# Mixture-of-experts stage: head reordered, down projection as three products of high and low parts, half of the output emptied by VectorE

## The chip, the cores and the metric

One Trainium2 (trn2) chip, one core. The time is that of one whole execution of the program on the device, in microseconds (us). Of the kernel before there are three timed runs, and one more execution that was profiled. All engines have in-order queues and meet at semaphores. TensorE (PE) multiplies, VectorE (DVE), ScalarE (ACT) and GpSimd (POOL) work elementwise, SyncE (SP) issues most of the DMAs.

## The reference

The model is a stack of blocks over 512 tokens of width 1024: a gated-delta mixer, a mixture of experts, sparse attention, a second mixture of experts, and two further layers. The change touches the mixture of experts alone, which runs twice. Its reference, cut down:

```python
def hier_moe(x, w_grp, b_grp, w_rt, b_rt, w_gate, w_up, w_down):
    xt = x.reshape(b * t, d)                        # 512 x 1024
    grp_p = softmax(xt @ w_grp + b_grp)             # 4 groups, the best one is taken
    grp_prob, grp_idx = lax.top_k(grp_p, 1)
    e_logits = ...                                  # 4 experts of that group
    top_p, top_i = lax.top_k(softmax(e_logits), 2)  # 2 of them per token
    gate = ...                                      # weight of each of 16 experts
    for wg, wu, wd, ge in experts:                  # 16 of them, hidden width 256
        hdn = silu(xt @ wg) * (xt @ wu)
        y += ge[:, None] * (hdn @ wd)
    return y
```

All of it is float32. The kernel computes an expert only for the tokens that chose it.

## The kernel before, in words

`stage_experts` runs a whole mixture-of-experts layer. The pairs (token, expert), 1,024 of them, are laid into **blocks** of 128 slots. Every expert has a block of its own, and more are added only for an expert with more than 128 tokens; in the profiled execution there are 16 blocks in each of the two layers (32 fetches of rows, 32 activations). So about half of the 2,048 slots hold no token.

**Head.** SP first issues the constants, the input weights of block 0 (two units of 1 MB), the store of h to `h_rows` in HBM (2 MB), the down weights of block 0 (1 MB) and the vectors `rt.loads` of the layer norm behind the stage. It then waits for `x_loaded[0]`, the rows of block 0, before it issues the weights of block 1 (L1873 to L1876). `Route.slots`, `rows`, `tables` and `tokens` on VectorE work out which token sits in which slot: PE multiplies one-hot rows (`in_row`, which lies in `rt.y`) with `named` (L1648) and so finds the token of every slot, and `tokens` turns that into row numbers `tok`. A slot without a token gets the number of some real row. After `tokens` VectorE makes the low parts of both weight units of block 0. GpSimd's `fetch` (L2023) copies one column of `tok` into `mine`, runs one further small operation, and issues an indirect DMA that brings 128 rows of 4 KB.

**Loop.** Five in-order queues run over the blocks (`pairs`: two unrolled, a loop of pairs, two at the end); buffers alternate by parity. A float32 product is made of three products in the format fp32r: x and w are each split in a high part (a copy by ScalarE that rounds to fp32r) and a low part (the rest, a subtraction), and PE adds xh wh + xh wl + xl wh. In the turn of block i the engines do, in this order:

- PE: 24 matmuls for gate and up of block i (L1951, `gu`), 8 transposes of the rows of block i+1 (L1930), the **down projection of block i-1** (L1942: 4 matmuls in plain float32, which the profile shows as 8 records), 2 transposes of the hidden layer of block i (L1964).
- ScalarE: the hidden layer of i-1 out of PSUM into `ht` (L1984), the high parts of the two weight units of block i+1 (L1789), silu (L2006), the high parts of the rows of i+1 (L1989), and the output of i-1 out of PSUM in two halves (`take`, L1996).
- VectorE: the low part of weight unit 0 of i+1 (L1793), the product of the hidden layer (L2071), the low parts of the rows of i+1 (L2062). Behind block 1 it also works out the gate weights and scales h (L2082).
- GpSimd: the fetch of rows two blocks ahead, and the low part of weight unit 1 of i+1 (L1793).
- SP: the output halves of block i to `moe_rows` (L1881), the down weights of i+2 (`store_and_load_down`, L1887), then the two input units of i+5 into the buffers that the low parts of i+3 have freed (`turn_over`, L1892).

The calls of SP's queue stand in this order in the loop:

```python
store(i)
sp.wait_ge(y_done, i(2, 2))
ws.load_down(sp, b, expert(i.plus(2)))
...
sp.wait_ge(ws.lo_ready[1], i(1, -1))
ws.load_in(sp, b, 1, e)
```

## Time and profile before

| what | value |
|---|---|
| three timed runs | 2580.58, 2588.68, 2588.92 us; median 2588.68 |
| the profiled execution | 2579.54 us, its span 2577.7 us, mean granted TensorE clock 0.948 |
| busy in the span | PE 90%, weight loads 70%, VectorE 45%, ScalarE 41%, GpSimd 33% |
| first expert layer | about 545 to 751 us of the span |
| second expert layer | about 1166 to 1371 us |
| HBM | 293.62 MB read, 31.60 MB written |

The two layers together are 16% of the span. The granted clock is given as a share of full speed (1.0 is 2.4 GHz, 0.5 is 1.2 GHz). A row of the timeline reads: start in us from the span's start, duration, engine, line, operation, output <- inputs, shape, count, and in brackets how long the engine had been idle and what ended that. "SPq" is the DMA queue of SyncE; its rows are issues, not transfers. Matmul records are modelled, so that the distance between starts tells the pace, not the duration of one.

### The profile page before, as it was taken

The page shows a single profiled execution, that of the slowest core. Times are in us where ns is not written, and L with a number is a line of the kernel's source. Part 1 is how long each engine was busy: PE and PEld are TensorE (multiplying, and loading weights), DVE is VectorE, ACT ScalarE, POOL GpSimd, SP SyncE. Part 2 cuts the span into 40 slices and gives each one's busy share as a digit, 9 for nine tenths or more (in the row PEclk, how much of TensorE's full clock was granted, in tenths as well). Part 3 has the DMA queues.
Part 4 walks back from the last instruction along what each step waited for, and adds up shares of the span by engine and source line. Part 5 has one row for each costly group of instructions (what it writes and reads, how often), then busy time and mean ns, then how long its engine had stood idle before and what let it go on. Part 6 is the DMA issues. An engine that isn't in the chain of part 4 may idle for free. (4 is left out here: it accounts for less than half of the span.)

```text
span 2577.7 us, 32698 instructions
## 1 busy us (share of the span) xinstructions
PE 2332.3 (90%) x12304; PEld 1810.2 (70%) x12304; DVE 1147.9 (45%) x2271; ACT 1047.9 (41%) x1830; POOL 853.7 (33%) x375
## 2 busy tenths in 40 slices
PE   6999999759969989995994899999997999999998
PEld 5888888656747866674763667678886767668886
DVE  3654642354436358754434453562223354462122
ACT  4443442216643247723664334533223334533222
POOL 2433532415552310023562222334332312224442
PEclk9999999769989999996997999999999999999999
DMA  6113110239983331017995311224222511315212
GB/s 138 49 50 115 42 50 30 90 137 393 401 296 84 135 105 44 30 51 261 396 406 191 102 49 62 90 67 147 97 66 76 172 33 50 119 50 164 98 66 74
DMA packets 190956, 327.15 MB, mean 127 GB/s; under 512 B 52544, under 2 KB 103056, under 8 KB 178528
## 3 DMA queue, kind: packets, MB, share of 16 engines
q1 hardware_dynamic: 183904, 300.08, 34.2%
q0 software_dynamic: 6912, 25.17, 2.6%
q8 instruction: 92, 1.51, 0.2%
q14 instruction: 48, 0.39, 0.0%
HBM read 293.62 MB, written 31.60 MB: 126 GB/s over the span
## 5 line engine op out<-in xcount | busy, mean ns | idle before, releaser
L159 POOL TENSOR_TENSOR branch_weights_wl<-branch_weights_wf,branch_weights_wh 128x2048 fp32r<-128x2048 f32 (+1 forms) x66 | 301.8, 4574 | 770.7 <-ACT branch_weights_wh L153 770.7
L153 ACT ACTIVATE branch_weights_wh<-branch_weights_wf 128x2048 fp32r<-128x2048 f32 (+1 forms) x66 | 124.6, 1889 | 200.2 <-PE merge_acc L207 92.9
L544 POOL TENSOR_TENSOR in_weights_wl<-in_weights_wf,in_weights_wh 128x1024 fp32r<-128x1024 f32 x32 | 79.5, 2486 | 237.1 <-ACT in_weights_wh L540 219.3
L207 PE MATMUL bmid_acc<-xh,branch_weights_wh 128*128 128x512 f32 x320 | 148.7, 465 | 9.1 <-PEq L72 9.1
L207 PE MATMUL merge_acc<-xh,branch_weights_wh 128*128 128x512 f32 x384 | 152.3, 397 | 3.4 <-PEq L72 3.4
L159 POOL TENSOR_TENSOR nsa_weights_wl<-nsa_weights_wf,nsa_weights_wh 128x2048 fp32r<-128x2048 f32 x13 | 59.5, 4585 | 282.2 <-ACT nsa_weights_wh L153 282.2
L207 PE MATMUL merge_acc<-xl,branch_weights_wh 128*128 128x512 f32 x384 | 152.1, 396 | 0.0
L207 PE MATMUL merge_acc<-xh,branch_weights_wl 128*128 128x512 f32 x384 | 152.0, 396 | 0.0
L207 PE MATMUL bmid_acc<-xh,branch_weights_wl 128*128 128x512 f32 x320 | 127.4, 398 | 0.0
L207 PE MATMUL bmid_acc<-xl,branch_weights_wh 128*128 128x512 f32 x320 | 127.3, 398 | 0.0
L1942 PE MATMUL exp_ps_y<-rt_wf,exp_ht 128*128 128x512 f32 x256 | 115.4, 594 | 2.9 <-ACT exp_ht L1984 1.9
L3274 ACT ACTIVATE bmid_pt<-bmid_x 128x256 f32<-128x256 f32 (+3 forms) x128 | 55.8, 436 | 141.6 <-PE bmid_x L3241 141.6
L568 PE MATMUL gmain_acc<-xh,in_weights_wh 128*128 128x512 f32 x256 | 110.6, 432 | 0.0
L1793 POOL TENSOR_TENSOR rt_wl<-rt_wf,rt_wh 128x2048 fp32r<-128x2048 f32 x16 | 76.9, 4804 | 79.8 <-ACT rt_wh L1789 79.8
L568 PE MATMUL gmain_acc<-xl,in_weights_wh 128*128 128x512 f32 x256 | 102.0, 398 | 0.0
L568 PE MATMUL gmain_acc<-xh,in_weights_wl 128*128 128x512 f32 x256 | 101.8, 398 | 0.0
L3611 ACT ACTIVATE merge_gate<-merge_acc,merge_gb 128x512 f32<-128x512 f32 x48 | 33.1, 689 | 148.8 <-DVE merge_merged L3639 75.2
L3637 DVE TENSOR_TENSOR merge_gate<-merge_gate,merge_b 128x512 f32<-128x512 f32 x32 | 22.0, 687 | 159.9 <-PE merge_b L3563 159.7
L207 PEld LDWEIGHTS merge_acc<-xh,branch_weights_wh 128*128 128x128 f32 x384 | 72.3, 188 | 21.3 <-issue 4.2
L1951 PE MATMUL exp_ps_gu<-rt_wh,xl 128*128 128x512 f32 x256 | 86.6, 410 | 0.4 <-DVE xl L2062 0.4
L207 PEld LDWEIGHTS merge_acc<-xh,branch_weights_wl 128*128 128x128 f32 x384 | 72.3, 188 | 17.3
L207 PEld LDWEIGHTS merge_acc<-xl,branch_weights_wh 128*128 128x128 f32 x384 | 72.4, 189 | 17.2
(659 smaller groups left out, 6209.0 us busy)
## 6 DMA issues: line engine op xcount, KB each, us to landing
branch_weights_wf<-w_in SPq DMA_DIRECT2D x56, 1024.0 KB, 5.1
rt_wf<-moe_w_out SPq DMA_DIRECT2D x32, 1024.0 KB, 10.2
rt_wf<-moe_w_in SPq DMA_DIRECT2D x32, 1024.0 KB, 9.2
in_weights_wf<-gdn_w_in SPq DMA_DIRECT2D x64, 256.0 KB, 3.4
nsa_weights_wf<-moe_w_in SPq DMA_DIRECT2D x16, 1024.0 KB, 9.9
moe_rows<-rt_y SPq DMA_DIRECT2D x64, 256.0 KB, 8.9
branch_weights_wf<-moe_w_in SPq DMA_DIRECT2D x16, 1024.0 KB, 9.8
merge_bwf<-w_branch SPq DMA_DIRECT2D x12, 1024.0 KB, 5.0
```

The lines of the kernel that those rows point to most:

```text
L153: act.activation(self.h[u][:, :, 0:self.cols(b)], self.s.f[u][:, :, 0:self.cols(b)], ACT.Copy).then_inc(self.s.hi_ready, 1)
L159: pool.tensor_tensor(self.l[u][:, :, 0:self.cols(b)], self.s.f[u][:, :, 0:self.cols(b)], self.h[u][:, :, 0:self.cols(b)].bitcast(F32), ALU ...
L207: mm = pe.matmul(self.acc[:, s, 0:cols], lhs[:, P * s:P * s + P], rhs, start=(u == 0 and k == 0 and n == 0), stop=(u == 1 and k == HALF - ...
L544: pool.tensor_tensor(self.l[n % 3][:], self.f[n % 3][:], self.h[n % 3][:].bitcast(F32), ALU.subtract).then_inc(self.lo_ready, 1)
L568: mm = pe.matmul(self.acc[:, tile % 3, :], w[n % 3][:, k, P * s:P * s + P], x[:, HALF * u + k, :], start=(u == 0 and k == 0 and m == 0), s ...
L1793: eng.tensor_tensor(self.l[b][u][:], self.f[b][u][:], self.h[b][u][:].bitcast(F32), ALU.subtract).then_inc(self.lo_ready[u], 1)
L1942: mm = pe.matmul(ps_y[:, c, :], ht[:, k, :], w[:, k, c, :], start=(k == 0), stop=(k == 1))
L1951: mm = pe.matmul(ps_gu[:, 0, :].rearrange("p (c n) -> p c n", c=2), x[:, HALF * u + k, :], ws.by_matrix(w[b][u])[:, :, k, :], start=(u == ...
L3274: act.activation(self.pt[:, e, 0:width], self.ps_t[:, 0:width], ACT.Copy).then_inc(self.copied, 1)
L3611: act.activation(gate[:, f % 2, :], ws.acc[:, f, :], ACT.Sigmoid, bias=gb[:, n, 4 * j + f:4 * j + f + 1]).then_inc(ws.evicted, 1)
L3637: dve.tensor_tensor(gate[:, f % 2, :], gate[:, f % 2, :], ps_b[:, f, :], ALU.mult).then_inc(b_out, 1)
```

## The change

1. **Route.** `in_row` and `named` are now fp32r tensors of their own, so that the eight matmuls that find the tokens run in fp32r. `tokens` gives a slot without a token the number 2T - 1, which no row has, and `fetch` passes `bounds_check=T - 1, oob_is_err=False`: such a slot is skipped. `xr` is set to zero once for this.
2. **Head.** SP issues the input weights of block 1 before the wait for `x_loaded[0]`, and both down loads and the norm vectors behind it. The first two fetches use `tok` itself as their offsets (`fetch_first`). VectorE makes the low part of weight unit 0 of block 0 before `tokens`, then `tokens`, then `tables`, then the low part of unit 1.
3. **Down projection.** `ht` becomes `hth` and `htl`, the down weights become `dh` (copied by ScalarE, `down_hi`) and `dl` (subtracted by VectorE, `down_lo`), both in the room of `g.xh`, one buffer for both parities. PE runs 12 fp32r matmuls where there were 4 in float32. `down_hi` of block i waits until the down projection of i-1 is done.
4. **Output.** ScalarE empties half 0, VectorE half 1.
5. **Waits.** The down load of i+2 waits for `dl_out` of block i instead of `y_done`, still behind `store(i)`. GpSimd's wait for `picked` counts two less, for the two fetches without it.

```diff
-        self.marks, self.in_row = marks, rt.y[:].rearrange("p (n r) -> p n r", r=P)
+        self.marks, self.in_row = marks, st.sb("in_row", [P, 2 * TT, P], F32R)
...
-        link(dve.tensor_scalar(self.spare[:], tok, 0.0, self.marks[:, P + n:P + n + 1], ALU.is_equal, ALU.mult))
+        link(dve.tensor_scalar(self.spare[:], tok, 0.0, 2.0 * T, ALU.is_equal, ALU.mult))
...
-                ws.load_down(sp, 0, 0)
+                for u in range(2):
+                    ws.load_in(sp, 1, u, 1)
+                sp.wait_ge(x_loaded[0], 16)
+                for b in range(2):
+                    ws.load_down(sp, b, b)
                 for x, src in rt.loads:
                     sp.dma_start(x, src).then_inc(ln_in, 16)
-                sp.wait_ge(x_loaded[0], 16)
-                for u in range(2):
-                    ws.load_in(sp, 1, u, 1)
-                ws.load_down(sp, 1, 1)
...
                 def store_and_load_down(i, b):
                     store(i)
-                    sp.wait_ge(y_done, i(2, 2))
+                    sp.wait_ge(dl_out, i(1, 1))
                     ws.load_down(sp, b, expert(i.plus(2)))
...
-                            mm = pe.matmul(ps_y[:, c, :], ht[:, k, :], w[:, k, c, :], start=(k == 0), stop=(k == 1))
+                            for m, (x, w) in enumerate(((hth, 0), (hth, 1), (htl, 0))):
+                                mm = pe.matmul(ps_y[:, c, :], x[:, k, :], by_k[w][:, k, c, :],
+                                               start=(k == 0 and m == 0), stop=(k == 1 and m == 2))
...
+                def down_hi(b, loads, i):
+                    act.wait_ge(ws.loaded[b][2], loads(16))
+                    if not i.is_first():
+                        act.wait_ge(y_done, i(2))
+                    act.activation(dh, ws.f[b][2][:], ACT.Copy).then_inc(dh_out, 1)
...
+                def fetch_first(b):
+                    pool.indirect_dma_start(xr[b][:], None, g.h_rows[:, :],
+                                            bass.IndirectOffsetOnAxis(route.tok[:, b:b + 1], 0),
+                                            bounds_check=T - 1, oob_is_err=False).then_inc(x_loaded[b], 16)
...
+                def hidden_lo(i):
+                    dve.wait_ge(hth_out, i(1, 1))
+                    dve.tensor_tensor(htl[:].rearrange("p k n -> p (k n)"), ps_t[:, 0, 0:HID],
+                                      hth[:].rearrange("p k n -> p (k n)").bitcast(F32), ALU.subtract).then_inc(htl_out, 1)
+
+                def down_lo(b, i):
+                    dve.wait_ge(dh_out, i(1, 1))
+                    dve.tensor_tensor(dl, ws.f[b][2][:], dh.bitcast(F32), ALU.subtract).then_inc(dl_out, 1)
+
+                def take(i):
+                    dve.wait_ge(y_done, i(2, 2))
+                    if not i.is_first():
+                        dve.wait_ge(y_stored[1], i(16))
+                    dve.tensor_copy(y[:, 512:D], ps_y[:, 1, :]).then_inc(y_out[1], 1)
...
                 def body(j, b, i, last):
+                    if not i.is_first():
+                        hidden_lo(i.plus(-1))
                     if not last:
                         ws.lo(dve, 1 - b, 0, i.plus(2))
...
+                    if not i.is_first():
+                        take(i.plus(-1))
+                    down_lo(b, i)
```

**Where instructions moved.** SyncE at the head of the first expert layer; `wf` and `rt_wf_0`, `rt_wf_1` are the input weights of blocks 0 and 1, `rt_wf_2` the down weights. Before:

```order
L1781 DMA nsa_weights_wf<-moe_w_in 128x2048
L1868 DMA h_rows<-h 128x4x1024
L1781 DMA nsa_weights_wf<-moe_w_in 128x2048
L1785 DMA rt_wf_2<-moe_w_out 128x2048
L1872 DMA nsa_weights_ln_vectors<-ln_ffn_g 128x1024
L1872 DMA nsa_weights_ln_vectors<-ln_ffn_b 128x1024
L1872 DMA nsa_weights_norm_gain<-by_feature 128x8
L1872 DMA nsa_weights_norm_shift<-by_feature 128x8
L1781 DMA rt_wf_0<-moe_w_in 128x2048
L1781 DMA rt_wf_1<-moe_w_in 128x2048
L1785 DMA rt_wf_2<-moe_w_out 128x2048
```

And of the change:

```order
L1781 DMA nsa_weights_wf<-moe_w_in 128x2048
L1870 DMA h_rows<-h 128x4x1024
L1781 DMA nsa_weights_wf<-moe_w_in 128x2048
L1781 DMA rt_wf_0<-moe_w_in 128x2048
L1781 DMA rt_wf_1<-moe_w_in 128x2048
L1785 DMA rt_wf_2<-moe_w_out 128x2048 x2
L1878 DMA nsa_weights_ln_vectors<-ln_ffn_g 128x1024
L1878 DMA nsa_weights_ln_vectors<-ln_ffn_b 128x1024
L1878 DMA nsa_weights_norm_gain<-by_feature 128x8
L1878 DMA nsa_weights_norm_shift<-by_feature 128x8
```

The wait for the first rows stands ahead of the row `x2` now; it stood ahead of `rt_wf_0`. Four issues of norm vectors moved behind it.

ScalarE in the turns of blocks 0 and 1, from the rows' high parts to the output (`xl` is the room of the rows' parts, L2006 and L2015 are silu). Before:

```order
L1989 ACTIVATE xl<-exp_ps_x 128x512 x2
L1984 ACTIVATE exp_ht<-exp_ps_t 128x256
L1789 ACTIVATE nsa_weights_wh<-nsa_weights_wf 128x2048 x2
L2006 ACTIVATE exp_act_g<-exp_ps_gu 128x256
L1989 ACTIVATE xl<-exp_ps_x 128x512 x2
L1996 ACTIVATE rt_y<-exp_ps_y 128x512 x2
```

And of the change:

```order
L1999 ACTIVATE xl<-exp_ps_x 128x512 x2
L1994 ACTIVATE xh<-rt_wf_2 128x2048
L1988 ACTIVATE exp_hth<-exp_ps_t 128x256
L1789 ACTIVATE nsa_weights_wh<-nsa_weights_wf 128x2048 x2
L2015 ACTIVATE exp_act_g<-exp_ps_gu 128x256
L1999 ACTIVATE xl<-exp_ps_x 128x512 x2
L2005 ACTIVATE rt_y<-exp_ps_y 128x512
L1994 ACTIVATE xh<-rt_wf_2 128x2048
```

The copy of the down weights, L1994, stands at the end of every turn, ahead of the hidden layer and of the high parts for the next block.

VectorE at the same place, from the low part for block 2 on. Before:

```order
L1793 TENSOR_TENSOR nsa_weights_wl<-nsa_weights_wf,nsa_weights_wh 128x2048
L2071 TENSOR_TENSOR exp_hid<-exp_act_g,exp_ps_gu 128x256
L2062 TENSOR_TENSOR xl<-exp_ps_x,xl 128x512 x2
L1755 TENSOR_REDUCE exp_sg<-exp_eg 128x4
L1756 SCALAR_TENSOR_TENSOR exp_sg<-exp_e,exp_sg 128x4
L1757 RECIPROCAL nsa_weights_weight<-exp_sg 128x4
L1758 TENSOR_TENSOR nsa_weights_weight<-nsa_weights_weight,exp_e 128x4
L2082 TENSOR_SCALAR h<-h 128x1024 x4
```

And of the change:

```order
L2088 TENSOR_TENSOR exp_htl<-exp_ps_t,exp_hth 128x256
L1793 TENSOR_TENSOR nsa_weights_wl<-nsa_weights_wf,nsa_weights_wh 128x2048
L2109 TENSOR_TENSOR exp_hid<-exp_act_g,exp_ps_gu 128x256
L2083 TENSOR_TENSOR xl<-exp_ps_x,xl 128x512 x2
L2099 COPY rt_y<-exp_ps_y 128x512
L2093 TENSOR_TENSOR xh<-rt_wf_2,xh 128x2048
L1755 TENSOR_REDUCE exp_sg<-exp_eg 128x4
L1756 SCALAR_TENSOR_TENSOR exp_sg<-exp_e,exp_sg 128x4
L1757 RECIPROCAL nsa_weights_weight<-exp_sg 128x4
L1758 TENSOR_TENSOR nsa_weights_weight<-nsa_weights_weight,exp_e 128x4
L2121 TENSOR_SCALAR h<-h 128x1024 x4
```

VectorE has three operations more in each turn, and the scaling of h now stands ahead of the low part of a hidden layer (L2088 of the next turn), on which PE's down projection waits.

## Rows read from the trace of the kernel before

**Rows 1.** The stretches view, 640 to 660: busy us per engine, clock, DMA share, GB/s.

```profile
640.00:660.00 20.00, 20.00 (x85) 13.99 (x84) 8.01 (x8) 13.10 (x16) 12.12 (x9) 1.00 1.02 416
```

**Rows 2.** The instructions in order of time: TensorE in one block's turn (start, us, engine, line).

```profile
641.57 0.48 PE L1951 MATMUL exp_ps_gu<-nsa_weights_wh,xl 128*128 128x512 f32 x1
...
647.16 1.03 PE L1930 MATMUL exp_ps_x<-ident,exp_xr 128*128 128x128 f32 x8
...
648.03 3.60 PE L1942 MATMUL exp_ps_y<-rt_wf,exp_ht 128*128 128x512 f32 x8
...
651.60 0.48 PE L1951 MATMUL exp_ps_gu<-rt_wh,xl 128*128 128x512 f32 x1
```

**Rows 3.** The same view, 548 to 590 us: the head of the first expert layer.

```profile
548.58 1.83 SPq L1872 DMA_DIRECT2D nsa_weights_ln_vectors<-ln_ffn_g  x1
...
564.60 0.18 DVE L1736 CAST exp_tok<-exp_spare 128x24 int32<-128x24 f32 x1
...
564.93 2.09 POOL L2024 TENSOR_TENSOR exp_mine<-exp_tok,exp_zero 128x1 int32<-128x1 int32 x1 [61.19 <-DVE exp_tok L1736]
...
569.40 1.12 POOL L2027 DMA_INDIRECT exp_xr<-h_rows,exp_mine  x1 [0.17 <-issue]
...
573.87 0.80 SPq L1781 DMA_DIRECT2D rt_wf<-moe_w_in  x2
...
576.52 0.77 PE L1951 MATMUL exp_ps_gu<-nsa_weights_wh,xl 128*128 128x512 f32 x1 [0.65 <-DVE xl L2062]
...
584.79 1.03 PE L1930 MATMUL exp_ps_x<-ident,exp_xr 128*128 128x128 f32 x8
584.91 1.91 ACT L1789 ACTIVATE rt_wh<-rt_wf 128x2048 fp32r<-128x2048 f32 x1 [1.67 <-DMA rt_wf<-moe_w_in]
...
586.98 4.53 POOL L1793 TENSOR_TENSOR rt_wl<-rt_wf,rt_wh 128x2048 fp32r<-128x2048 f32 x1 [9.47 <-ACT rt_wh L1789]
588.14 0.38 ACT L2006 ACTIVATE exp_act_g<-exp_ps_gu 128x256 f32<-128x256 f32 x1
...
589.88 0.76 PE L1951 MATMUL exp_ps_gu<-rt_wh,xl 128*128 128x512 f32 x1 [0.22 <-DVE xl L2062]
```

**Rows 4.** The same view, TensorE, second expert layer: the end of its first block.

```profile
1203.94 1.03 PE L1930 MATMUL exp_ps_x<-ident,exp_xr 128*128 128x128 f32 x8
```

**Rows 5.** The same view, ScalarE, second expert layer: the first activation.

```profile
1208.54 0.38 ACT L2006 ACTIVATE exp_act_g<-exp_ps_gu 128x256 f32<-128x256 f32 x1
```

**Rows 6.** The same view, 599 to 603 us, VectorE: scaling of h behind block 1.

```profile
600.03 2.50 DVE L2082 TENSOR_SCALAR h<-h 128x1024 f32<-128x1024 f32 x4
```

**Rows 7.** The same view, 636 to 651 us: the other engines in one block's turn.

```profile
636.05 4.84 POOL L1793 TENSOR_TENSOR nsa_weights_wl<-nsa_weights_wf,nsa_weights_wh 128x2048 fp32r<-128x2048 f32 x1 [3.66 <-ACT nsa_weights_wh L1789]
...
641.04 0.33 SPq L1781 DMA_DIRECT2D nsa_weights_wf<-moe_w_in  x1
...
642.12 0.38 ACT L1984 ACTIVATE exp_ht<-exp_ps_t 128x256 f32<-128x256 f32 x1
...
642.39 3.72 ACT L1789 ACTIVATE rt_wh<-rt_wf 128x2048 fp32r<-128x2048 f32 x2
...
643.65 0.36 SPq L1785 DMA_DIRECT2D rt_wf<-moe_w_out  x1
...
644.34 2.29 DVE L1793 TENSOR_TENSOR rt_wl<-rt_wf,rt_wh 128x2048 fp32r<-128x2048 f32 x1 [4.66 <-ACT rt_wh L1789]
...
646.19 4.86 POOL L1793 TENSOR_TENSOR rt_wl<-rt_wf,rt_wh 128x2048 fp32r<-128x2048 f32 x1 [3.77 <-ACT rt_wh L1789]
```

**Rows 8.** DMA issues of the page: bytes each and median us from issue to landing.

```profile
branch_weights_wf<-w_in SPq DMA_DIRECT2D x56, 1024.0 KB, 5.1
rt_wf<-moe_w_out SPq DMA_DIRECT2D x32, 1024.0 KB, 10.2
```

**Rows 9.** The instructions in order of time: the last two down projections of the first expert layer.

```profile
739.22 3.67 PE L1942 MATMUL exp_ps_y<-rt_wf,exp_ht 128*128 128x512 f32 x8 [1.05 <-issue]
...
743.95 3.67 PE L1942 MATMUL exp_ps_y<-rt_wf,exp_ht 128*128 128x512 f32 x8 [0.84 <-ACT exp_ht L1984]
```

60 lines of the change are left out of this document (34 added, 26 removed).

## Prediction, made before the change was run

> **What bounds the kernel now.** I read the page first, for the place of the two expert layers in the span; then the stretches view inside one of them; then the instructions in order of time through one turn of the loop, through the head and through the tail. Blocks are counted from 0.
>
> In the loop two things are full at once. TensorE is busy in 20.00 of 20 us at granted clock 1.00, that is 2.4 GHz, and the DMA share is 1.02 at 416 GB/s [rows 1]. A turn of TensorE is 10.03 us, from one first matmul to the next: 5.59 us for the 24 fp32r matmuls, 0.87 for the transposes, 3.57 for the down projection with the two transposes behind it [rows 2]. From the down projection of block 5 (648.03) to that of block 14 (739.22) are 9 turns: 10.13 us each [rows 2, 9]. TensorE waits for nothing there, so it sets the turn. The DMAs do not lag enough to be waited for, but a down load takes 10.2 us to land [rows 8], where a load of the same size in a calmer stage takes 5.1 [rows 8].
>
> In the head TensorE waits for a chain: `tok` at 564.78; a copy of one column on GpSimd that lasts 2.09 us, beside VectorE's low part; the fetch, issued at 569.40; SP, which waited for the rows, issues at 573.87; first matmul at 576.52. Block 1 waits for its weights, issued only at 573.87: the second high part begins at 584.91, silu at 588.14, gate and up of block 1 at 589.88, though those of block 0 had ended at 584.79 [rows 3].
>
> **The change, part by part.**
>
> *Rows of block 0.* Route in fp32r shortens the token matmuls, but VectorE puts a low part of 2.29 us [rows 7] between them and `tokens`, and saves waiting instead: `tok` comes some 0.8 us earlier at most. The two small GpSimd operations go: the fetch is issued with `tok`, near 564.1 instead of 569.40. The queue is empty then (the same 6 MB lie ahead as before). I take 5.3 us.
>
> *Weights of block 1.* They are issued some 25 us earlier and land before the rows do, so their high parts hide beside block 0. Gate and up of block 0 end at 584.79 - 5.3 = 579.5, silu is over 0.6 later at 580.1; before at 588.52 [rows 3]. Gain 8.4 us. Second layer: 1203.94 - 5.3 + 0.6 = 1199.2 against 1208.92 [rows 4, 5], gain 9.7. I take the table load ahead of silu as hidden; if not, 1.3 less each. **Head: -18.1 us.** SP pays: down loads and norm vectors are issued behind the wait; one norm issue takes 1.83 us [rows 3]. The weights of block 2 therefore go out at the time they do now, and are not late.
>
> *Behind block 1.* VectorE now does `down_lo` (2.29) and the scaling (2.50 [rows 6], and about 0.8 of small operations before it) ahead of the low part of the hidden layer (about 0.4), all behind ScalarE's `down_hi` (1.91 for this shape [rows 3]): 7.9 us from the end of the last down projection. TensorE is ready for the next after 6.5 (5.59 + 0.87 and a transpose [rows 2]). A stall of 1.4 us in each layer: **+2.8**. It has no cover any more; before, nobody waited for the scaling.
>
> *The matmuls themselves.* 12 fp32r matmuls at 5.59/24 = 0.233 us are 2.80, in place of about 3.43: 0.63 off a turn, so TensorE alone would turn in 9.4 us. Less is fetched too: half of the slots, some 0.26 MB of 4.2 a turn.
>
> *The ring that the loop becomes.* This is the term that decides. The down load of i+2 still stands behind `store(i)`, but is wanted earlier: `down_hi` of i+2 comes right after the down projection of i+1, a turn later, where TensorE wanted it nearly two turns later. Behind `down_hi` on ScalarE stand the hidden layer and both high parts for block i+4; behind those GpSimd's low part; behind that on SP the input load, the next stores, the next down load but one. One way round is two turns:
> - from the end of GpSimd's low part (636.05 + 4.84 = 640.89) to the issue of the down load (643.65): 2.76 [rows 7];
> - its landing L;
> - `down_hi` 1.91, `down_lo` 2.29, low part of the hidden layer 0.4, VectorE's low weights 2.29: 6.9. ScalarE's second high part is ready already at 1.91 + 0.27 + 3.72 = 5.9 [rows 7];
> - GpSimd's low part: 4.53 alone [rows 3].
>
> If GpSimd can start only when VectorE's is over, the ring is 14.1 + L. The rows say so: begun 0.44 us before VectorE's ends, it takes 4.86, 0.33 more than alone [rows 3, 7], and the copy of one column took 2.09 [rows 3]. L: ahead of and with the down load lie an input load, two stores, a fetch and itself, 2.9 MB, at 416 GB/s [rows 1] 6.9 us from the input load's issue at 641.04, 2.6 us before the down load's [rows 7]; 4.3 remain, and a fixed part of at most 5.1 - 2.5 = 2.6 [rows 8]; I take 2.0. L = 6.3, nearest to the calm 5.1. The turn is (14.1 + 6.3)/2 = 10.2, against 10.13: over 14 turns and two layers **+2**. The 0.63 that TensorE saves is lost in the ring.
>
> The Trainium skill, in SBUF - State Buffer, section "Who interferes with whom", speaks against this change: a VectorE instruction with two SBUF inputs and a GpSimd instruction that reads SBUF exclude each other for the whole instruction, and the change adds one of 2.29 us a turn. By the rule the ring is the 14.1 + L above; without it (GpSimd starting at 5.9 and taking 4.53) 13.1 + L, a turn of 9.7 and a time some 14 us shorter. The trace agrees with the rule, with the 2.09 us.
>
> *Tail.* The last down projection follows the one before by 1.06 us (743.95 after 739.22 + 3.67) [rows 9]. Now `down_hi`, `down_lo` and the hidden low part stand between: 4.6 and about 0.2 of handing over, +3.7; both projections are shorter by some 0.8, but one of these lies in the turn already counted: +3.7 - 1.6 = **+2.1** a layer, **+4.2**.
>
> The second `take` moves to VectorE, which has room; it gives ScalarE back a part of `down_hi`. I cost it at nothing: TensorE's own work hides it. VectorE was busy 8.01 of 20 us [rows 1].
>
> **Sum:** -18.1 + 2.8 + 2 + 4.2 = about -9. The profiled execution took 2579.54, so 2570.5; the median of the runs shown is 9.1 above that execution. Against the median: 2588.7 - 9 = **2580**. A measurement here can tell about 0.3%, 8 us, from no change, so the sum lies on that edge.
>
> **Bounds of the unknown.** L from 5.1 to 10.2 [rows 8]. At 5.1 the turn is 9.6. At 10.2 it would be 12.1, but that landing belongs to a queue that is always full; a slower ring empties it. I hold L = 8.3, half-way up, for the far end: 11.2.
>
> **Rivals.**
> - *The ring opens.* L about 5.1, TensorE nearly sets the turn at 9.6: 28 turns save 15 us where I add 2. -26, **2563**. For it: less is fetched, and the queue has gaps. Against: the load is issued right behind an input load and two stores.
> - *Late down loads: slower than before.* L = 8.3 makes the turn 11.2, 28 x 1.07 = +30 instead of +2: +19, **2608**. ScalarE would stand at `down_hi` for the DMA in every second turn, and everything behind it. The whole is slower from a turn of 10.13 + 11/28 = 10.5, that is L = 6.9. For it: the 10.2 of now; against: the demand falls from 4.2 to 3.9 MB a turn.
> - *Slots aren't skipped.* If the fetch moves all 128 rows whatever the bound, L grows by 0.6 and the turn by 0.3: +9, **2588**, no change. The packets of the fetch tell it.
>
> **Chances.** The forecast 0.42, on the edge: half faster by over 0.3%, half within, a little slower. The ring opens 0.22. Late loads 0.22. Not skipped 0.08, within. The rest 0.06, a clock that falls in the new pauses of TensorE among it (it is granted 1.00 now [rows 1]), slower. So faster 0.43, same 0.28, slower 0.29. The forecast's own range, with L from 5.8 to 6.9, is 2573 to 2588. The range for 8 in 10 reaches into both rivals: 2562 to 2606.
>
> **What would show it.** Right: first matmul of an expert layer 5 us earlier, silu of block 0 8 to 10 earlier; a down projection of 12 records in about 2.8 us; ScalarE's copy of the down weights idle before it, released by the DMA, for 1 to 2 us in many turns; TensorE waiting before the down projection for the low part of the hidden layer or of the weights; turns near 10.2, perhaps alternating; DMA share below 1.0; GpSimd's low part near 5 us; about 4.8 us before the last down projection. Wrong: `down_hi` never waits for a DMA, or a turn far from 10.2, or a head gain under 6 us a layer.

## The result, and the profile after

| | us | 95% interval of the ratio |
|---|---|---|
| before, median of 4 runs beside the change | 2588.48 (2580.58 to 2588.92) | |
| after, median of 4 runs | 2630.39 (2624.99 to 2633.58) | 1.0167 (1.0141 to 1.0193) |
| after, the profiled execution | 2630.14, span 2628.3, mean clock .942 | |

The change makes the kernel slower by 42 us, 1.7%. The forecast was 2580, the range 2562 to 2606: both were wrong, and the sign with them.

To find the place I cut each expert layer at four kinds of record: the issue of the load of `marks` (the stage begins), the first silu, the fourth and the sixteenth, and the copy into `exp_mx`, which waits for the last store (the stage ends). In the first layer of the kernel before, two of them are these, in the view of the instructions in order of time (start us, duration us, engine, line, operation, tiles; in brackets the idle time before and what ended it); the silu are those of the same form as in [rows 3, 5]:

```profile
545.30 0.35 SPq L1866 DMA_DIRECT2D exp_marks<-c_marks  x1
...
750.55 0.15 DVE L2086 COPY exp_mx<-exp_tm 128x1 f32<-128x1 f32 x1 [11.51 <-DMA moe_rows<-rt_y]
```

And after the change:

```profile
548.40 0.35 SPq L1868 DMA_DIRECT2D exp_marks<-c_marks  x1
...
581.34 0.39 ACT L2015 ACTIVATE exp_act_g<-exp_ps_gu 128x256 f32<-128x256 f32 x1 [2.88 <-PE exp_ps_gu L1955]
...
599.85 0.39 ACT L2015 ACTIVATE exp_act_g<-exp_ps_gu 128x256 f32<-128x256 f32 x1 [0.47 <-PE exp_ps_gu L1955]
...
618.32 0.39 ACT L2015 ACTIVATE exp_act_g<-exp_ps_gu 128x256 f32<-128x256 f32 x1
...
754.03 0.38 ACT L2015 ACTIVATE exp_act_g<-exp_ps_gu 128x256 f32<-128x256 f32 x1
...
776.06 0.15 DVE L2127 COPY exp_mx<-exp_tm 128x1 f32<-128x1 f32 x1 [2.26 <-DMA moe_rows<-rt_y]
```

Differences of such starts give the account, here for both layers (first / second, us):

| | head: to silu of block 0 | block 0 to 3 | block 3 to 15 | tail | stage |
|---|---|---|---|---|---|
| before | 42.8 / 42.1 | 29.0 / 29.4 | 121.1 / 121.1 | 12.3 / 11.2 | 205.2 / 203.8 |
| after | 32.9 / 33.5 | 37.0 / 34.3 | 135.7 / 138.5 | 22.0 / 19.8 | 227.7 / 226.1 |
| sum over both layers | -18.5 | +12.9 | +32.0 | +18.3 | +44.8 |

So the head gained what it was to gain, and three other places lost more than three times that. (The +44.8 is between the two profiled executions, which are 50.6 apart. The other 5.8 us lie outside the two layers, 3.1 of them ahead of the first one. The profiled execution before was 9 under its median, the one after was at its own.)

**The loop.** The stretches view (busy us of PE, PEld, DVE, ACT, POOL with counts, granted clock, DMA share, GB/s) after the change, against [rows 1]:

```profile
640.00:660.00 20.00, 18.02 (x82) 13.86 (x81) 10.56 (x12) 11.06 (x14) 13.46 (x8) 1.00 0.97 359
660.00:680.00 20.00, 16.09 (x78) 12.52 (x77) 14.09 (x14) 13.92 (x16) 10.34 (x5) 1.00 0.95 330
680.00:700.00 20.00, 17.06 (x80) 13.03 (x79) 11.54 (x10) 14.08 (x15) 10.39 (x9) 1.00 0.96 343
```

TensorE no longer fills its time, though its clock is at 1.00 (2.4 GHz), and the DMA share is nearly what it was while the rate fell from 416 to 330 to 359 GB/s. The view of waits, 620 to 745 us (total us, times, longest), names the new wait:

```profile
ACT xh L1994 <- DMA rt_wf<-moe_w_out: 35.2, 11, 3.8
DVE xh L2093 <- ACT xh L1994: 33.1, 9, 3.8
```

ScalarE stands in front of the high part of the down weights (L1994, `down_hi`) for the DMA, 3.2 us at each of 11 waits. One way round, in order of time; the low part that frees the input tile, the issues, the wait, and what then follows on ScalarE, VectorE and GpSimd:

```profile
640.40 5.38 POOL L1793 TENSOR_TENSOR nsa_weights_wl<-nsa_weights_wf,nsa_weights_wh 128x2048 fp32r<-128x2048 f32 x1 [3.36 <-ACT nsa_weights_wh L1789]
...
641.46 4.81 SPq L1781 DMA_DIRECT2D nsa_weights_wf<-moe_w_in  x2
...
646.47 0.90 SPq L1883 DMA_DIRECT2D moe_rows<-rt_y  x2
...
648.43 0.35 SPq L1785 DMA_DIRECT2D rt_wf<-moe_w_out  x1
...
658.72 1.93 ACT L1994 ACTIVATE xh<-rt_wf 128x2048 fp32r<-128x2048 f32 x1 [3.38 <-DMA rt_wf<-moe_w_out]
...
660.68 2.29 DVE L2093 TENSOR_TENSOR xh<-rt_wf,xh 128x2048 fp32r<-128x2048 f32 x1 [3.79 <-ACT xh L1994]
...
663.22 2.28 DVE L1793 TENSOR_TENSOR nsa_weights_wl<-nsa_weights_wf,nsa_weights_wh 128x2048 fp32r<-128x2048 f32 x1
...
664.60 5.38 POOL L1793 TENSOR_TENSOR nsa_weights_wl<-nsa_weights_wf,nsa_weights_wh 128x2048 fp32r<-128x2048 f32 x1 [5.47 <-ACT nsa_weights_wh L1789]
```

From 645.78 to the issue at 648.43 are 2.65; from `down_hi` at 658.72 to the end of GpSimd's low part at 669.98 are 11.26. That is 13.9 us of work in the ring, where the prediction had 14.1. The page gives the landing:

```profile
rt_wf<-moe_w_in SPq DMA_DIRECT2D x32, 1024.0 KB, 8.5
rt_wf<-moe_w_out SPq DMA_DIRECT2D x32, 1024.0 KB, 8.7
```

(13.9 + 8.7)/2 = 11.3. The ten turns from silu of block 4 to that of block 14 (629.54 to 743.91) took 11.44 each in the first layer, and 11.75 in the second. Where turns of a run are given below, they are this mean, for the first and the second layer; before the change it was 10.19 and 10.09.

The trace's packet records tell what the landing is made of. For the 20 down loads of these turns, the median landing is 8.9 us, and 3.25 MB begin to move on all queues between issue and landing, at 358 GB/s.

**Behind block 1.** VectorE in the first layer, against [rows 6], and GpSimd beside it:

```profile
599.52 7.27 DVE L2121 TENSOR_SCALAR h<-h 128x1024 f32<-128x1024 f32 x4
606.71 0.41 DVE L2088 TENSOR_TENSOR exp_htl<-exp_ps_t,exp_hth 128x256 fp32r<-128x256 f32 x1
```

```profile
601.12 4.51 POOL L1793 TENSOR_TENSOR rt_wl<-rt_wf,rt_wh 128x2048 fp32r<-128x2048 f32 x1
```

The four scalings take 7.27 us and not 2.50: all of GpSimd's 4.51 lies inside them. The low part of the hidden rows of block 1 (L2088), for which TensorE's down projection waits, comes behind. The silu of blocks 2 and 3 are 18.5 us apart, 10.1 before. The Trainium skill, in SBUF - State Buffer, section "Who interferes with whom", names this case beside the one that the prediction used: `tensor_scalar` in a two-port mode also excludes GpSimd, and whoever issues first keeps the shared ports for its whole instruction. The rows agree, 2.50 + 4.51 = 7.0 against 7.27.

While TensorE waits there its granted clock falls: .83 in 600 to 620, where it was 1.00 before. What this costs is not separated from the wait.

```profile
600.00:620.00 20.00, 13.44 (x58) 10.77 (x57) 17.12 (x15) 9.19 (x11) 9.38 (x6) 0.83 0.81 280
```

**The tail** of the first layer, against [rows 9]: ScalarE, GpSimd, VectorE and TensorE.

```profile
754.29 3.71 ACT L153 ACTIVATE nsa_weights_wh<-nsa_weights_wf 128x2048 fp32r<-128x2048 f32 x2
...
756.28 9.04 POOL L159 TENSOR_TENSOR nsa_weights_wl<-nsa_weights_wf,nsa_weights_wh 128x2048 fp32r<-128x2048 f32 x2 [6.82 <-ACT nsa_weights_wh L153]
...
756.57 1.22 PE L1945 MATMUL exp_ps_y<-xh,exp_hth 128*128 128x512 f32 x2 [3.92 <-DVE exp_htl L2088]
...
762.10 1.91 ACT L1994 ACTIVATE xh<-rt_wf 128x2048 fp32r<-128x2048 f32 x1 [1.88 <-PE exp_ps_y L1945]
...
764.04 3.43 DVE L2093 TENSOR_TENSOR xh<-rt_wf,xh 128x2048 fp32r<-128x2048 f32 x1 [1.16 <-ACT xh L1994]
...
767.86 1.22 PE L1945 MATMUL exp_ps_y<-xh,exp_hth 128*128 128x512 f32 x2 [5.47 <-DVE exp_htl L2088]
```

The two down projections begin 11.3 us apart, 4.7 before. Three things add up: the first of them waited 3.92 (it then runs mostly at half clock, 1.2 GHz: 5.3 us for 12 matmuls that take 2.9 in the loop), `down_hi` may begin only when it has ended, since there is one pair of tiles for the parts, and `down_lo` takes 3.43 behind GpSimd's two low parts for the next stage. The last product is mostly at half clock too: it follows 5.47 us in which TensorE did nothing, and the granted clock of 740 to 760 is .88 and that of 760 to 780 is .67:

```profile
740.00:760.00 20.00, 14.78 (x60) 11.24 (x59) 10.00 (x10) 12.30 (x14) 9.09 (x2) 0.88 0.73 258
760.00:780.00 20.00, 7.52 (x19) 5.21 (x18) 5.30 (x5) 4.28 (x5) 6.74 (x4) 0.67 0.20 64
```

### The profile page after: what moved, and what is told of

The parts are those of the page before. It is cut to its first block and busy times, and to the rows that moved or that the text cites. A ratio compares the mean times of both kernels' runs of the same rounds, so it can differ in the third digit from the quotient of the medians.

```text
span 2628.3 us, 33054 instructions
## 1 busy us (share of the span) xinstructions
PE 2334.9 (89%) x12416; PEld 1838.3 (70%) x12416; DVE 1257.3 (48%) x2367; ACT 1083.5 (41%) x1830; POOL 871.9 (33%) x371
## 5 line engine op out<-in xcount | busy, mean ns | idle before, releaser
L1945 PE MATMUL exp_ps_y<-xh,exp_hth 128*128 128x512 f32 x256 | 91.7, 442 | 50.2 <-DVE exp_htl L2088 50.2
L2093 DVE TENSOR_TENSOR xh<-rt_wf,xh 128x2048 fp32r<-128x2048 f32 x32 | 79.0, 2468 | 98.8 <-ACT xh L1994 87.1
L1793 POOL TENSOR_TENSOR rt_wl<-rt_wf,rt_wh 128x2048 fp32r<-128x2048 f32 x16 | 83.3, 5203 | 59.1 <-ACT rt_wh L1789 59.1
L1945 PEld LDWEIGHTS exp_ps_y<-xh,exp_hth 128*128 128x128 f32 x256 | 50.8, 209 | 67.2 <-DVE exp_htl L2088 32.3
L3652 ACT ACTIVATE merge_gate<-merge_acc,merge_gb 128x512 f32<-128x512 f32 x48 | 33.1, 690 | 148.7 <-DVE merge_merged L3680 75.2
L1994 ACT ACTIVATE xh<-rt_wf 128x2048 fp32r<-128x2048 f32 x32 | 61.4, 1917 | 77.5 <-DMA rt_wf<-moe_w_out 72.1
```

The lines of the kernel that those rows point to most:

```text
L1793: eng.tensor_tensor(self.l[b][u][:], self.f[b][u][:], self.h[b][u][:].bitcast(F32), ALU.subtract).then_inc(self.lo_ready[u], 1)
L1945: mm = pe.matmul(ps_y[:, c, :], x[:, k, :], by_k[w][:, k, c, :], start=(k == 0 and m == 0), stop=(k == 1 and m == 2))
L1994: act.activation(dh, ws.f[b][2][:], ACT.Copy).then_inc(dh_out, 1)
L2093: dve.tensor_tensor(dl, ws.f[b][2][:], dh.bitcast(F32), ALU.subtract).then_inc(dl_out, 1)
L3652: act.activation(gate[:, f % 2, :], ws.acc[:, f, :], ACT.Sigmoid, bias=gb[:, n, 4 * j + f:4 * j + f + 1]).then_inc(ws.evicted, 1)
```

## The experiments

Twelve kernels ran, in three groups; each group has its own runs of the kernel before (medians 2586.45 for experiments 1, 2, 6 and 8, 2585.2 for 4, 5, 9 and 10, 2582.85 for 3, 7, 11 and 12), which its ratios refer to. The change has its own too, 2588.48. So a difference of medians between two groups can be off by some us, and where it is small the ratios are given beside it. My theory after the first reading was the ring through the down load with its landing at 8.7. The rival was the memory path: the loop might be bound by a rate of some 340 GB/s, whatever waits where. A second question was why the rate had fallen.

### 1. Head alone

The head, the fetch and the order of the first loads of the change, with the down projection, the emptying and the issue of the down load of before.

```diff
-                def down(i):
-                    pe.wait_ge(htl_out, i(1, 1))
-                    pe.wait_ge(dl_out, i(1, 1))
...
+                def down(b, loads, i):
+                    pe.wait_ge(ht_out, i(1, 1))
+                    pe.wait_ge(ws.loaded[b][2], loads(16))
...
-                    sp.wait_ge(dl_out, i(1, 1))
+                    sp.wait_ge(y_done, i(2, 2))
```

> The changed kernel with its head (route order, in_row and named_r in F32R, order of the first loads, fetch_first, skipping of empty slots) but with the down projection, the emptying of its result and the issue of the down load of before (fp32 matmuls, both halves emptied by ScalarE). Prediction of the sum for this part: head -18.1 us over two layers against the kernel before, 2588 - 18 = 2570 us, turn 10.1 us. Theory A (the head's gain is there, all the loss comes from the down projection in three products): 2568 to 2573 us and a turn of 10.1. Theory B (skipping or the new order of loads slows the weights in the loop too): turn 10.4 to 11.4, 2577 to 2590 us, and a rate in 640 to 660 well under 416 GB/s.

Measured: 2573.07 us, ratio 0.9941 (0.9922 to 0.9961), 13.4 less than before. The time is at the upper end of theory A, but the turns, 10.4 and 10.7, are those of theory B, and so is the rate of 378 GB/s in 640 to 660. The head (to the silu of block 0) took 33.2 and 33.1 us, as in the full change: -18.6. Blocks 3 to 15 took 122.4 and 124.8 against 121.1 each, which gives 5.0 back; blocks 0 to 3 and the tails give back 3.4 more. What makes the loop longer here was not tested. In 640 to 660 TensorE is full again:

```profile
640.00:660.00 20.00, 20.00 (x85) 13.92 (x84) 8.00 (x8) 12.09 (x17) 12.36 (x8) 1.00 1.00 378
```

So nearly all of the loss comes with the down projection in three products and what it asks of the other engines. By difference that half of the change costs 2630.4 - 2573.1, some 57 us.

### 2. The down load between the two input loads

```diff
 def store_and_load_down(i, b):
     store(i)
-    sp.wait_ge(dl_out, i(1, 1))
-    ws.load_down(sp, b, expert(i.plus(2)))
...
+def load_down(i, b):
+    e = expert(i)
+    sp.wait_ge(dl_out, i(1, -1))
+    ws.load_down(sp, b, e)
...
 def turn_over(i, b):
     e = expert(i)
     sp.wait_ge(ws.lo_ready[0], i(1, -1))
     ws.load_in(sp, b, 0, e)
+    if not (isinstance(i.base, int) and i() < 4):
+        load_down(i.plus(-2), b)
     sp.wait_ge(ws.lo_ready[1], i(1, -1))
     ws.load_in(sp, b, 1, e)
...
```

> The changed kernel with one edit on SP's queue: the load of the down weights for a block is issued between the two input loads of a turn (after u = 0 of two blocks later) instead of behind the stores of y at the end of a turn, about half a turn earlier; it still waits for the low part of the down weights that frees its buffer. Theory A (the ring: ScalarE's high part waits for the down load, the load is issued only after VectorE's low part, two blocks go round in 14.1 us of work plus 8.7 us of landing): with the landing taken off the ring ScalarE's wait for rt_wf at L1994 (35.2 us in the stretch 620 to 745) goes to under 5, and the turn falls from 11.44 to 9.8 us or less, where TensorE's products and the engines' chain bound it; ten turns in each of two layers give -25 to -35 us, 2600 us or a little less. Theory B (the memory path: at 330 to 359 GB/s the 3.15 MB of weights and 0.3 MB of rows and results that a turn moves need 10.5 to 11 us whatever their order): the wait only changes its place, to the input loads, and the turn stays between 10.8 and 11.4; 2618 to 2630 us.

Measured: 2601.48 us, ratio 1.0068 (1.0046 to 1.0091): 29 less than the change (26 by the ratios), where theory A said 25 to 35. But its turn of 9.8 or less did not come: 10.8 and 10.6 us. Of theory A the first half held (ScalarE's wait for `rt_wf` is gone), of theory B the end ("the wait only changes its place"), though not to the input loads. The waits of 640 to 740:

```profile
ACT rt_y L2013 <- DMA moe_rows<-rt_y: 33.3, 10, 3.6
DVE rt_y L2107 <- DMA moe_rows<-rt_y: 24.1, 9, 3.0
```

ScalarE now waits 3.3 us a turn to empty its half of the output, because the store of the block before has not landed: there is one tile y, and its store stands in SP's queue behind the loads. `down_hi` and the next high parts stand behind it on ScalarE.

### 3. The down load ahead of the stores

```diff
 def store_and_load_down(i, b):
-    store(i)
+    e = expert(i.plus(2))
     sp.wait_ge(dl_out, i(1, 1))
-    ws.load_down(sp, b, expert(i.plus(2)))
+    ws.load_down(sp, b, e)
+    store(i)
```

> The changed kernel with one edit on SP's queue: in each turn the down load is issued ahead of the two stores of y and not behind them. Theory A (the turn is half of a ring of 14.1 us of work and the landing L; L is the time that the bytes ahead of the down load in the queue take: an input load not yet begun, two stores, the rows and itself, 2.9 MB at about 340 GB/s = 8.5 us): 0.5 MB less stands ahead, and the issue comes about 1.0 us earlier, so L = 7.2 and the ring is shorter by 1 to 2.5 us: a turn of 10.3 to 10.9 us, 2603 to 2617 us. What could take it back is the store of y, which is then behind another 1 MB. Theory B (only the sum of the bytes counts): a turn of 11.4, 2626 to 2634 us.

Measured: 2628.14 us, ratio 1.0177 (1.0161 to 1.0192), turns of 11.6 and 11.2: no gain, the number of theory B. (The profiled execution, 2620.93, is the fastest of its four.) The waits of 640 to 740 say that B's reason isn't the right one:

```profile
ACT rt_y L2006 <- DMA moe_rows<-rt_y: 36.2, 9, 4.8
DVE rt_y L2100 <- DMA moe_rows<-rt_y: 30.6, 9, 4.2
```

No wait for the down load is left; a wait for the store of y of the same size stands in its place. This is the taking back that the expectation named, and it took all. I read from this that the loop of the change has **two rings** through SP's queue, one through the down load and one through the store of y, nearly equal in length, and that which of the two is issued first decides only which is waited for. The two runs that follow open the second. The Trainium skill, in DMA: Bandwidth & Descriptors, section "Queues, rings and completion order", states that each DMA engine consumes the descriptors of a queue in ring order. The landings agree: a store of 256 KB took 7.3 us in the change and 8.8 here, behind one load of 1 MB more. (At the 340 GB/s of the loop its own bytes would take under 1 us, an estimate.)

### 4. Down parts before the emptying

The run of experiment 2, and on ScalarE and VectorE:

```diff
-                    if not i.is_first():
-                        take(i.plus(-1))
                     down_hi(b, j.plus(1), i)
+                    if not i.is_first():
+                        take(i.plus(-1))
```

> The run with the down load between the two input loads, and one further edit: ScalarE makes the high part of the down weights, and VectorE the low part, before they empty their halves of the output and not after. There ScalarE waited 33.3 us and VectorE 24.1 us in 640 to 740 for the store of y to land (longest 3.6), with the high part of the down weights (1.91 us) and the next weights' high parts queued behind it. Theory A (the turn of 10.6 to 10.8 us hangs on that wait in front of ScalarE's conversions, since the stores stand behind 2 to 3 MB of loads in SP's queue): with 1.9 us of work put ahead of the wait the turn falls to 9.8 to 10.2 us, 2585 to 2592 us. Theory B (the memory path moves about 4.0 MB a turn at 365 to 377 GB/s and its engines are at .98 to 1.00): the turn stays within 0.15 us of 10.7, 2598 to 2604 us.

Measured: 2584.62 us, ratio 0.9997 (0.9981 to 1.0013), turns of 10.1 and 10.0. Theory A. 17 us less than experiment 2 for two statements in another order; the wait for y remains, 16.2 us in place of 33.3, but now other work is done ahead of it.

### 5. A second tile y

The run of experiment 2 with `y = [rt.y, st.sb("y2", [P, D])]`, used by turns, and the waits for the stores counted for each tile.

> The run with the down load between the two input loads, and a second tile y used by turns (so that a block's result waits for the store of two blocks before), with the parts of the down weights after the emptying as before. Theory A (wait for the store of y bounds the turn): ScalarE's and VectorE's waits for moe_rows<-rt_y vanish, and the turn falls from 10.7 to 9.6 to 10.0 us, where TensorE and the low parts on GpSimd bound it: 2580 to 2588 us. Theory B (memory path): the waits go over to the loads of the weights and the turn stays 10.5 to 10.8: 2596 to 2604 us.

Measured: 2581.80 us, ratio 0.9992 (0.9976 to 1.0007), turns of 9.9 and 10.0 in the profiled execution, which is the slowest of its ten; many are 9.4 to 9.5, TensorE's own length. Theory A. The waits for the store are gone from the view of 640 to 740. A wait of ScalarE for the down load is back in it, 12.8 us in 6 turns, so the ring through that load still shows at times. Theory B, the memory path as the bound at 340 to 377 GB/s, falls with this and the last run: both moved 386 to 409 GB/s in 640 to 700.

### 6. No slot is skipped

```diff
-        link(dve.tensor_scalar(self.spare[:], tok, 0.0, 2.0 * T, ALU.is_equal, ALU.mult))
+        link(dve.tensor_scalar(self.spare[:], tok, 0.0, self.marks[:, P + MAX_BLOCKS - 1:P + MAX_BLOCKS], ALU.is_equal, ALU.mult))
...
-                                            bass.IndirectOffsetOnAxis(mine[b][:], 0),
-                                            bounds_check=T - 1, oob_is_err=False)
+                                            bass.IndirectOffsetOnAxis(mine[b][:], 0))
```

> The changed kernel, but slots without a token are given the number of a spare token, as before, and the fetches have no bound on the row number, so every fetch moves all of its 128 rows. The computation is unchanged. Theory A (skipping is what slows the packets of the weights: 109 packets over 450 ns in 640 to 740 before, 370 after): the rate in the loop returns to about 416 GB/s, the down load lands in 5 to 6.5 us, and the turn is 10.1 to 10.4 us: 2605 us. Theory B (the slow packets come with the order and the bunching of the loads, not with skipping): the fetch moves 24 MB instead of 16, the rate stays at 340 to 360 GB/s in the loop, the landing stays at 8.5 us or more and the turn at 11.4 or longer: 2630 to 2645 us.

Measured: 2629.93 us, ratio 1.0174 (1.0151 to 1.0198), not to be told from the change (2630.39). Theory B, at its lower end. Turns were 12.0 and 11.7, and the rate in the three stretches of 20 us from 640 to 700 was 367, 355 and 319 GB/s. The page's line of the fetch queue shows that the bound does what it says, in packets, MB and share, first here, then in the change:

```profile
q0 software_dynamic: 6912, 25.17, 2.6%
```

```profile
q0 software_dynamic: 6912, 16.79, 1.8%
```

A third of the bytes goes, and not one packet: in the packet records of this queue 2,048 packets of 4,096 bytes, the empty slots of two layers, have become packets of 4 bytes. It brings nothing that can be measured here.

### 7. A plain load in place of the fetch

```diff
-                    pool.indirect_dma_start(xr[b][:], None, g.h_rows[:, :],
-                                            bass.IndirectOffsetOnAxis(mine[b][:], 0),
-                                            bounds_check=T - 1, oob_is_err=False).then_inc(x_loaded[b], 16)
+                    pool.dma_start(xr[b][:], g.h_rows[0:P, :]).then_inc(x_loaded[b], 16)
```

> The changed kernel, but from the third block on the rows of a block aren't gathered: a plain load of the first 128 rows takes the place of the indirect one (the values of the output are others, the work on them the same; 0.52 MB a block where the fetch that skips moves 0.27). Theory A (the weights' packets are slow in the 4 us after GpSimd issues an indirect load, since it makes its descriptors then): under 100 packets over 450 ns in the hundred us of the loop instead of 370, a rate of 380 GB/s or more, a turn of 10.6 to 11. Theory B (the slow packets come when the queue of the loads has run low and fills again, as the runs with a turn of 9.6 to 10 us, which have 90 to 140 of them, suggest): 300 or more remain, and the turn is 11.4 or more.

Measured: 2631.27 us, ratio 1.0188 (1.0173 to 1.0204), turns of 11.7 and 11.7, and 281 packets of weights over 450 ns in 640 to 740. The turn is theory B's. Of the packets neither number is reached: fewer than 300, far from under 100. The indirect load isn't what makes most of the packets slow.

### 8. Without the scaling of h

```diff
-                    for t in range(TT):
-                        dve.tensor_scalar(g.h[:, t, :], g.h[:, t, :], ALPHA, None, ALU.mult)
```

> The changed kernel without VectorE's four scalings of h by ALPHA in the second turn of each layer (so the residual that is added behind the experts is not scaled; its time alone is read). Theory A (the scalings, 7.27 us while GpSimd makes its low part, hold back VectorE's low part of the hidden rows and with it the down projection, ScalarE's high part and the next silu): the silu of the third to the fourth block, 18.5 us apart, come to 11 to 12, which is -7 us in each layer, 2617 us. Theory B (the stall there is set by the weights, which land late in the slow burst at 600 to 610, and by TensorE's clock of .83): 17 us or more remain between the two silu, and the time falls by under 3 us.

Measured: 2622.12 us, ratio 1.0156 (1.0127 to 1.0185), by the medians 8 less than the change, between the two theories (-13 and -3). By the ratios (1.0167 for the change) it is 3, and the intervals overlap; the stages of the profiled executions are 4.8 shorter, 3.1 of it in blocks 0 to 3. The silu of blocks 2 and 3 are 15.9 and 16.4 apart: theory A's 11 to 12 did not come, nor B's 17. The row of VectorE's low part of the next weights tells what holds the rest:

```profile
600.60 6.21 DVE L1793 TENSOR_TENSOR rt_wl<-rt_wf,rt_wh 128x2048 fp32r<-128x2048 f32 x1
```

```profile
600.06 4.59 POOL L1793 TENSOR_TENSOR rt_wl<-rt_wf,rt_wh 128x2048 fp32r<-128x2048 f32 x1
```

GpSimd began 0.54 us earlier, ended at 604.65, and VectorE ended 2.2 us later, its usual 2.28. In the change the scalings were drawn out beside GpSimd's low part; without them it is the next operation of VectorE with two SBUF inputs that is held until GpSimd ends.

### 9. The scaling in the head

```diff
                 ws.lo(dve, 0, 1, BlockCount(1))
+                route.weights(dve)
+                dve.wait_ge(h_kept, 16)
+                for t in range(TT):
+                    dve.tensor_scalar(g.h[:, t, :], g.h[:, t, :], ALPHA, None, ALU.mult)
```

> The changed kernel with the scaling of h by ALPHA (four operations on VectorE) and the weights of the experts moved from behind the second block into the head, ahead of the first block's low parts, where VectorE waits for the first rows to land. The computation is unchanged. Theory A (7.27 us of scaling are off the path, but the low part of the next weights is then held by GpSimd's low part, as in the run without scaling): as that run, 2620 to 2624 us, silu of the third to the fourth block 15.9 and 16.4 apart instead of 18.5 and 17.1. Theory B (in the head the scaling delays the first block's low parts as much as it saves): 2626 to 2632 us. A third way: with the weights' four small operations out of the way as well, VectorE reaches its low part before GpSimd starts its own, and is not held: silu 11 to 13 apart, 2613 to 2618 us.

Measured: 2621.47 us, ratio 1.0141 (1.0110 to 1.0173). The number is theory A's, the silu of blocks 2 and 3 (12.5 and 12.5 apart) are those of the third way, and the head costs nothing (33.4 and 33.6). Blocks 0 to 3 took 30.1 and 29.7 instead of 37.0 and 34.3, that is -11.5. VectorE's low part now ends before GpSimd begins its own:

```profile
597.82 2.28 DVE L1793 TENSOR_TENSOR rt_wl<-rt_wf,rt_wh 128x2048 fp32r<-128x2048 f32 x1
```

```profile
601.01 4.61 POOL L1793 TENSOR_TENSOR rt_wl<-rt_wf,rt_wh 128x2048 fp32r<-128x2048 f32 x1
```

But blocks 3 to 15 took 144.5 and 139.5 instead of 135.7 and 138.5, +9.8: nearly all of what the stall gave came back as longer turns, and no run shows why. (The stage sums are 453.1 against 453.8. The median is 9 lower all the same; but the ratios are 1.0141 and 1.0167, with intervals that overlap, so a gain in time is not shown.)

### 10. The last down projection in one fp32 product

```diff
-                _, last = pairs(pe, body)
-                down(last)
+                loads, last = pairs(pe, body)
+                pe.wait_ge(hth_out, last(1, 1))
+                pe.wait_ge(ws.loaded[1][2], loads(16))
...
+                    for k in range(2):
+                        mm = pe.matmul(ps_y[:, c, :], ht[:, k, :], w[:, k, c, :], start=(k == 0), stop=(k == 1))
```

> The changed kernel, but the down projection of the last block alone is one fp32 product from the loaded weights, as before the change (no high and low part of its weights, no low part of its hidden rows). Theory A (the tail, 22.0 us from the last silu to the end of the stage against 12.3 before, is the chain down product of the block before, high part 1.9, low part 3.4 behind GpSimd's low parts, low part of the hidden rows, product at half clock): 6 to 8 us less in each layer, 2615 to 2619 us. Theory B (the tail is late because the down load and the product of the block before are late; the last product starts only little earlier and runs 3.7 us in fp32 at whatever clock): under 3 us a layer, 2625 us or more.

Measured: 2614.91 us, ratio 1.0120 (1.0082 to 1.0158): 15.5 less than the change by the medians, 12 by the ratios, 14.5 in the stages of the profiled executions. Theory A. The tails took 14.6 and 10.9 us instead of 22.0 and 19.8. The last product starts as soon as the hidden rows are copied:

```profile
762.58 3.70 PE L1979 MATMUL exp_ps_y<-rt_wf,exp_ht 128*128 128x512 f32 x8 [0.47 <-ACT exp_ht L2038]
```

### 11 and 12. All together

Experiments 2, 4, 5, 9 and 10 in one kernel, and the same without 4.

> All together: the changed kernel with the down load between the two input loads, the parts of the down weights made before the output is emptied, a second tile y, the scaling of h in the head, and the last block's down projection as one fp32 product. From the runs: 2582 with the second tile y; the scaling took 5 us off the silu of the third to the fourth block in each layer, -8 to -10; the fp32 product at the end took 15 off, of which 10 to 15 remain. If these add up: 2560 us (2555 to 2566), 1% below the kernel before. If TensorE's turn of 9.4 or the memory path gives a part of it back: 2566 to 2576.

> As the run with all together, but with the outputs emptied before the parts of the down weights are made, as in the changed kernel. With two tiles y nobody waits for a store, so the order should matter little: within 4 us of the other, 2556 to 2568 us. If emptying late holds back TensorE's next down projection, this one is the faster by 3 to 8 us.

Measured: 2553.50 us with all, ratio 0.9889 (0.9872 to 0.9906); 2556.96 without the edit of experiment 4, ratio 0.9893 (0.9877 to 0.9908). The parts add up to a little more than was expected (2555 to 2566). The order of the parts and the emptying makes 3.5 us with two tiles y, within the 4 that were expected and not to be told apart; it made 17 with one. Both beat the kernel before, by 29 and 26 us, and the change by over 70. With all, the account of the two stages is:

| | head | block 0 to 3 | block 3 to 15 | tail | stage |
|---|---|---|---|---|---|
| all together | 33.5 / 33.5 | 28.1 / 27.0 | 117.4 / 117.1 | 11.6 / 11.4 | 190.7 / 189.0 |

409.0 - 379.7 = 29.3 us, as much as the medians differ. (The two profiled executions are 26.0 apart, so 3.3 us go the other way outside the layers.) The scaling in the head and the opened rings go together here: blocks 0 to 3 keep their gain. The turns are 9.9 and 9.8. The stretches view shows TensorE at 19.89 of 20 us, the DMA share at 1.00 and GpSimd at 18.76:

```profile
640.00:660.00 20.00, 19.89 (x96) 15.70 (x95) 15.97 (x16) 15.25 (x16) 18.76 (x9) 1.00 1.00 393
```

GpSimd's queue is nearly closed. Its low parts start 9.8 us apart, a turn, and between 620 and 720 it neither works nor issues for only about 1 us a turn. Part of its time is waiting inside its own instructions, as the copy of one column shows, which takes 0.19 us alone. That GpSimd is the next limit is argued from these rows; no run tests it.

```profile
658.15 5.77 POOL L1793 TENSOR_TENSOR rt_wl<-rt_wf,rt_wh 128x2048 fp32r<-128x2048 f32 x1
663.89 2.23 POOL L2060 TENSOR_TENSOR exp_mine<-exp_tok,exp_zero 128x1 int32<-128x1 int32 x1
...
667.96 5.78 POOL L1793 TENSOR_TENSOR nsa_weights_wl<-nsa_weights_wf,nsa_weights_wh 128x2048 fp32r<-128x2048 f32 x1
```

## Why the prediction was wrong, and where it was right

- **Head, -18.1: right.** -18.5 in the profiles, -18.6 in experiment 1. That the sum fits so well is partly luck: the layers gave -9.9 and -8.6, where -8.4 and -9.7 were said, and the two misses cancel. `tok` starts 566.27 - 548.40 = 17.9 us into the stage, before 19.3, so 1.4 earlier and not 0.8; the fetch stands 5.0 earlier, where 5.3 was taken; the table load is hidden, since ScalarE waits 2.88 us for TensorE behind it. In the change:

```profile
566.27 0.18 DVE L1736 CAST exp_tok<-exp_spare 128x24 int32<-128x24 f32 x1
...
567.46 1.17 POOL L2034 DMA_INDIRECT exp_xr<-h_rows,exp_tok  x1 [16.92 <-DVE exp_tok L1736]
```

- **12 matmuls of 0.233 us: right.** In the change the twelve records of one projection lie between 650.64 and 653.54, and many turns of the opened loop of experiment 5 take 9.4 to 9.5, the length that was given for TensorE alone.

```profile
650.64 0.72 PE L1945 MATMUL exp_ps_y<-xh,exp_hth 128*128 128x512 f32 x2 [0.82 <-DVE exp_htl L2088]
...
653.54 0.38 PE L1968 MATMUL exp_ps_t<-ident,exp_hid 128*128 128x128 f32 x2
```

- **The ring: the mechanism was right, and the size of one term failed.** Work was 13.9 against 14.1, and the turn is half of work and landing. **L was the step that failed**: 6.3 was taken, 8.7 was measured. The term was built from two parts.

  The first part was the bytes: 2.9 MB from the issue of the input load on, at 416 GB/s, of which 2.6 us were taken as gone before the down load is issued. They were not gone. 3.25 MB began to move between the down load's issue and its landing. The input load ahead of it had itself stood behind the first input load, issued 4.5 us earlier. In the 6.8 us (median) that the second takes to land, 2.15 MB begin to move, twice its own size. And the bytes moved at 358 GB/s and not at 416. At 416 the 3.25 MB would take 7.8 us, so 1.3 of the landing is the rate (an estimate).

  The second part, a fixed 2.0 us on top, isn't needed: 3.25/0.358 is 9.1 already, against a median landing of 8.9 for these loads.

  I named 8.3 as the far end, with a turn of 11.2, and gave it 0.22. The calm 5.1, from which I took the low value as near, was never near: in every profile whose view gives it, the median landing of the down load in the layers is 7.9 us or more, also in the opened loops (9.5 on the page of experiment 5). They turn faster since the load is issued earlier, not since it lands sooner. The argument that a slower ring empties the queue was wrong in this: a queue with gaps was also a slower one.

  Over the 12 turns from block 3 to 15 in two layers the loss is +32.0, where all turns together were costed at +2. Not all of it is the ring's: experiment 1, which has no such ring, loses 5.0 there.
- **A second ring was not seen.** "The second `take` moves to VectorE [...] I cost it at nothing." What it missed is on ScalarE and VectorE alike: emptying waits for the store of the block before, and `down_hi` is behind it. In the change this wait is mostly covered by the one for the down load (5.6 us in 640 to 740 on ScalarE, against 29.5 for the load); experiments 2 and 3 show it alone, 3.3 to 4.0 us a turn.
- **The stall behind block 1, +2.8: undersized.** Blocks 0 to 3 lost 12.9. The order of the operations was right; the scaling was costed at 2.50 [rows 6], and in its new place it runs beside a low part of GpSimd and takes 7.27. I had used the exclusion of the two engines for the ring and not here. Leaving the scaling out gives only 3.1 of the 12.9 back, since the next operation is then held (experiment 8); moving it to the head gives 11.5 (experiment 9).
- **The tail, +4.2: undersized.** 18.3. The chain was named, but at the durations of the loop: `down_lo` took 3.43 and not 2.29, both products ran at half clock mostly, and the down load of block 14 was late (3.57 us of wait). Experiment 10, which takes the chain away for the last block, shortens the two tails by 16.3. The sum has a slip as well: it says that one of the two shorter projections is already counted in the turn, and takes both off, 0.8 a layer.
- **Slots skipped: right that they are, and worth nothing.** The rival had 9 us for them by a longer L; experiment 6 shows no difference in the time (2629.93 against 2630.39).

The rival "late down loads", 2608, was the true case in kind, and the range of 8 in 10 left even it out. With the loop's measured +32 in place of its +30, and the two undersized terms, it is -18 + 32 + 13 + 18 = +45 in the profiled executions.

## What to carry to other kernels

When a change makes a tile's use earlier, ask for every DMA in that queue what stands ahead of it at its issue, in bytes that have not yet moved, and write down each ring that closes through it: also the stores. Swapping two issues next to each other in one queue only changed which ring was waited for. An earlier issue opened one (29 us from one load issued half a turn earlier); a second output tile opened the other (20 more), and so, nearly as well, did work put ahead of the wait (17 more). A duration may be moved to another place only with its neighbours: 2.50 us became 7.27 beside GpSimd.
